# Decoder block with a PEER expert layer: gate factors applied by ScalarE, the search's small tables in PSUM, all 128 dot products in the first table stage

## The chip, the cores and the metric

The kernel runs on one core of one Trainium2 chip. The metric is the device time of one execution in microseconds, as the median of several runs; lower is better.

## What is computed

One layer for 512 tokens of width 1024, all in float32: RMSNorm, a combined projection, two mixers (HGRN2 and forgetting attention), a gated merge, and then the PEER layer, which the change touches:

```python
q = (xt @ w_q).reshape(T, PEER_HEADS, 2, PEER_DK_HALF)            # 8 heads, 2 halves
s = jnp.einsum('thpd,hpnd->thpn', q, sub_keys)                    # 128 keys per half
s1, i1 = lax.top_k(s[:, :, 0], 16)
s2, i2 = lax.top_k(s[:, :, 1], 16)
cand = (s1[..., :, None] + s2[..., None, :]).reshape(T, PEER_HEADS, 256)
cand_idx = (i1[..., :, None] * 128 + i2[..., None, :]).reshape(T, PEER_HEADS, 256)
top_s, pos = lax.top_k(cand, 16)
idx = jnp.take_along_axis(cand_idx, pos, axis=-1)                 # 16 of 16384 experts per head
gates = jax.nn.softmax(top_s, axis=-1)
a = jax.nn.gelu(jnp.einsum('cd,ced->ce', xc, u_table[ic]), approximate=False) * gc
y = jnp.einsum('ce,ced->cd', a, v_table[ic])                      # 128 experts per token
```

The result is h + y, normalised once more.

## The kernel before, in words

Four blocks follow one another, each closed by a barrier of all engines: the projections and mixers (to about 390 us), the merge and the queries of the search (to 600 us), **the first table stage** (to about 1285 us) and **the value stage** (to the end).

The tokens are in four tiles of 128. For three of them (384 tokens, `DT`) the PEER layer is dense: all 16384 experts are computed. In the first table stage TensorE goes through the table `u` in 128 *chunks* of 128 experts; chunk `j` is 24 products of 384 columns (`unit_product`, L212 to L214: every float32 operand is split into a high and a low part, and three products are summed per 128 rows). A unit of 512 KB is loaded by the SP queue into one of four buffers (`load_unit`), ScalarE copies out its high part (`split_hi`, L203), GpSimd subtracts to get the low part (`split_lo`, L207), four chunks ahead of TensorE (`LEAD`); the buffer of a chunk's split is that of the chunk that has just ended. ScalarE applies the gelu (L1169) and stores the result to memory. In the value stage the gelus times the dense gates are multiplied with the table `v`, again in 128 chunks; there VectorE makes the low parts.

The *dense gates* (for each token a 128x128 table of the 16 x 8 selected experts with their gates) are also made in the first table stage, in 96 *quads* of four tokens. For one token it is a product of two one-hot tables of 128 slots by 128 keys: `hot` (first key index) and `hotg` (second index, times the gate). VectorE makes both (`quads`, L1217 and four times L1223), comparing `iota` (0 to 127, in PSUM bank 3) with the indices in `slot_t`; TensorE multiplies them (L1380) right behind the chunk that `quad_chunk(q)` names; ScalarE moves the result out (L1177) and stores it in batches of eight quads (`dense_d`). Four quads can be under way (`HOTS`).

Where `slot_t` comes from is the *search* on VectorE. `retrieve_pair` does two heads of a tile: top 16 of four lists of 128 keys, the sums of candidates, top 16 of these, then the ranks (`rank`, L1281, L1282, and L1284 to `rank_f`), a comparison of ranks against `iota` (`pick`, L1286), its product with the key numbers (`key_f`, written by L1271, read by L1292) and a sum. There are 16 such *pairs*, four for each of the four tiles. After each tile ScalarE takes the exponential (at chunk `EXP_AT`), VectorE normalises (`normalise`), TensorE transposes (at chunk `SLOTS_AT`), and VectorE copies to `slot_t` (`slots_out`).

The fourth tile (the first one that is searched) is sparse: its 128 tokens gather their own 128 rows of `u` and 128 rows of `v` (`gather`, an indirect DMA from GpSimd's queue, L1046, 512 KB each, into six buffers). A *dot* (`u_dot`, L1055) multiplies one row buffer with the tokens' vectors, which stand in PSUM (`x_rows`), and sums up; a row of `v` is added by `add_row` in the value stage. 104 dots run in the first table stage (`DOTS_U`), 24 in the value stage, on a copy of the vectors in SBUF (`xs`). The gelu and the gates of the first 96 come at the end of the first stage, the rest at chunks 26 and 30 of the value stage.

The order of all this is written out by hand. Dots and quads are filled in between the dependent steps of a pair (`fill`; the numbers per pair are `PAIR_DOTS` and `PAIR_QUADS`), and the rest stands behind the last pair as a tail of two quads and two dots in turn. Gather `g` is issued by GpSimd behind its split of chunk `GATHER_AT[g]`. At chunk `MIX_AT` the SP queue loads the first two parts of what the value stage needs (`mix`).

## Time and profile before

| | us |
|---|---|
| median of 3 runs | 1870.97 |
| lowest, highest | 1869.51, 1871.16 |
| the profiled execution's own time | 1871.95 |
| its span, first to last instruction | 1870.1 |
| TensorE busy | 1766.6 (94%) |
| VectorE busy | 1327.5 (71%) |
| GpSimd busy | 821.1 (44%) |
| ScalarE busy | 669.9 (36%) |

The busy time of TensorE is modelled, since products are pipelined, so 94% is not nearness to its peak. The shares are means over stages with different limits, and the views by stretch tell more. "Idle before" stands with the instruction that ended the idle time, and with what it waited for. PEclk is the share of full TensorE clock (2.4 GHz) that was granted.

### The profile page before, as it was taken

To read this page: it belongs to the slowest core of one execution; us is meant where nothing else is said; L and a number is where in the kernel's file an instruction comes from. 1 tells how busy PE (TensorE), PEld (TensorE's weight loads), DVE (VectorE), ACT (ScalarE), POOL (GpSimd) and SP (SyncE) were. 2 spreads that over 40 slices of the span, in tenths; PEclk is the share of its full clock that TensorE was granted. 3 is DMA by queue.
4 is the path that set the end of the run, shared out by engine and by line. 5 is a ranking of instruction groups with operands and counts; after the bars stand their busy time and mean duration, and the time that the engine had idled before them with its cause. 6 is when DMAs were issued, how large, how long until landed. Compare 5 with 4: busy or idle time off the path is not lost. (4 is left out here: it accounts for less than half of the span.)

```text
span 1870.1 us, 25727 instructions
## 1 busy us (share of the span) xinstructions
PE 1766.6 (94%) x9603; PEld 1628.3 (87%) x9603; DVE 1327.5 (71%) x2720; ACT 669.9 (36%) x993; POOL 821.1 (44%) x478
## 2 busy tenths in 40 slices
PE   6998999999999999999999879885999999999997
PEld 4887876677788999989999878785999999999996
DVE  6467452644432699999999957761788888888885
ACT  4343333443321334334343324232333333333332
POOL 4432222234342787866555446454233334344420
PEclk8999999999999999999999989897999999999999
DMA  6322222255344788967677558777899999999991
GB/s 182 93 76 60 79 80 68 68 161 148 101 131 126 235 284 287 299 227 265 239 269 269 184 215 330 263 273 265 314 369 376 370 375 365 371 367 379 372 346 46
DMA packets 260844, 436.09 MB, mean 233 GB/s; under 512 B 14960, under 2 KB 184176, under 8 KB 259056
## 3 DMA queue, kind: packets, MB, share of 16 engines
q1 hardware_dynamic: 203696, 249.87, 41.0%
q0 software_dynamic: 36864, 134.23, 18.8%
q10 hardware_dynamic: 20160, 50.34, 7.3%
q8 instruction: 77, 1.26, 0.3%
q14 instruction: 47, 0.39, 0.1%
HBM read 373.57 MB, written 60.82 MB: 232 GB/s over the span
## 5 line engine op out<-in xcount | busy, mean ns | idle before, releaser
L207 POOL TENSOR_TENSOR spl_a<-raw,spl_a 128x1024 fp32r<-128x1024 f32 x172 | 419.4, 2439 | 477.2 <-ACT spl_a L203 472.8
L203 ACT ACTIVATE spl_a<-raw 128x1024 fp32r<-128x1024 f32 x296 | 313.1, 1059 | 538.2 <-PE bank L214 422.4
L212 PE MATMUL bank<-act,spl_a 128*128 128x384 f32 (+1 forms) x1216 | 433.1, 356 | 12.5 <-DVE act L480 7.7
L213 PE MATMUL bank<-act,spl_a 128*128 128x384 f32 (+1 forms) x1216 | 422.8, 348 | 0.0
L214 PE MATMUL bank<-act,spl_a 128*128 128x384 f32 (+1 forms) x1216 | 422.4, 347 | 0.0
L1046 POOL DMA_INDIRECT rows<-in_v_tab,expert x128 | 173.7, 1357 | 261.7 <-DVE acc L1498 231.4
L212 PE MATMUL bank<-aws,spl_a 128*128 128x384 f32 x768 | 260.4, 339 | 20.3 <-DVE aws L1484 20.3
L213 PE MATMUL bank<-aws,spl_a 128*128 128x384 f32 x768 | 260.2, 339 | 0.0
L214 PE MATMUL bank<-aws,spl_a 128*128 128x384 f32 x768 | 260.1, 339 | 0.0
L212 PEld LDWEIGHTS bank<-act,spl_a 128*128 128x128 f32 x1216 | 233.1, 192 | 24.7 <-issue 12.2
L213 PEld LDWEIGHTS bank<-act,spl_a 128*128 128x128 f32 x1216 | 233.0, 192 | 7.9 <-issue 1.0
L214 PEld LDWEIGHTS bank<-act,spl_a 128*128 128x128 f32 x1216 | 232.3, 191 | 8.2
L207 DVE TENSOR_TENSOR spl_a<-raw,spl_a 128x1024 fp32r<-128x1024 f32 x124 | 151.8, 1224 | 79.5 <-ACT spl_a L203 79.3
L1055 DVE SCALAR_TENSOR_TENSOR rows<-rows,x_rows 128x1024 f32<-128x1024 f32 x104 | 125.2, 1210 | 60.1 <-DMA rows<-in_u_rows,expert 59.9
L1046 POOL DMA_INDIRECT rows<-in_u_rows,expert x128 | 130.3, 1018 | 79.8 <-DVE rows L1055 59.3
L212 PEld LDWEIGHTS bank<-aws,spl_a 128*128 128x128 f32 x768 | 144.8, 189 | 20.6 <-issue 20.6
L207 POOL TENSOR_TENSOR spl_b<-raw,spl_b 128x1024 fp32r<-128x1024 f32 x37 | 90.4, 2449 | 163.3 <-ACT spl_b L203 163.3
L1498 DVE SCALAR_TENSOR_TENSOR acc<-rows,a_row,acc 128x1024 f32<-128x1024 f32 x126 | 159.1, 1279 | 0.0
L1452 ACT ACTIVATE aws<-aw 128x384 fp32r<-128x384 f32 x128 | 67.3, 526 | 228.8 <-DVE aw L1478 228.8
L214 PEld LDWEIGHTS bank<-aws,spl_a 128*128 128x128 f32 x768 | 144.8, 189 | 0.0
L213 PEld LDWEIGHTS bank<-aws,spl_a 128*128 128x128 f32 x768 | 144.8, 188 | 0.0
L1380 PE MATMUL bank<-hotg,hot 128*128 128x128 f32 x768 | 106.0, 289 | 37.2 <-DVE hotg L1223 37.2
(281 smaller groups left out, 2878.3 us busy)
## 6 DMA issues: line engine op xcount, KB each, us to landing
raw<-in_u_t SPq DMA_DIRECT2D x128, 512.0 KB, 4.1
raw<-in_v_tab SPq DMA_DIRECT2D x128, 512.0 KB, 7.2
gelu_ux<-gl ACTq DMA_DIRECT2D x128, 192.0 KB, 4.7
dense_gates<-mixbuf ACTq DMA_DIRECT2D x12, 2048.0 KB, 7.6
mixbuf<-dense_gates SPq DMA_DIRECT2D x32, 768.0 KB, 9.9
mixbuf<-gelu_ux SPq DMA_DIRECT2D x32, 768.0 KB, 12.6
raw<-in_w_in SPq DMA_DIRECT2D x45, 512.0 KB, 3.9
raw<-in_w_q SPq DMA_DIRECT2D x16, 512.0 KB, 4.0
```

Source lines behind the costliest of these rows:

```text
L203: eng.activation(spl(n, 0, slice(0, W)), raw[:, s, :], ACT.Copy).then_inc(hi_done, 1)
L207: eng.tensor_tensor(spl(n, 1, slice(0, W)), raw[:, n % RAW, :], spl(n, 0, slice(0, W)).bitcast(F32), ALU.subtract).then_inc(lo_done, 1)
L212: nc.tensor.matmul(out, w_hi, x_hi, start=first, stop=False)
L213: nc.tensor.matmul(out, w_hi, x_lo, start=False, stop=False)
L214: return nc.tensor.matmul(out, w_lo, x_hi, start=False, stop=last)
L1046: pool.indirect_dma_start(out=rows[:, g % ROWS, :], out_offset=None, in_=u_rows[:, :] if g < SLOTS else v_rows, in_offset=bass.IndirectOff ...
L1055: dve.scalar_tensor_tensor(out=row, in0=row, scalar=1.0, in1=x, op0=ALU.mult, op1=ALU.mult, accum_out=z_row[:, g:g + 1]).then_inc(row_used, 1)
L1380: ins = nc.tensor.matmul(bank[4 + q % 2][:, t * P:(t + 1) * P], hot[:, q % HOTS, t, :], hotg[:, q % HOTS, t, :], start=True, stop=True)
L1452: act_e.activation(aws[:, 0, j % 4, :], aw[:, j % 2, :], ACT.Copy).then_inc(a_hi, 1)
L1498: dve.scalar_tensor_tensor(out=acc[:, s % 2, :], in0=row, scalar=a_row[:, s:s + 1], in1=acc[:, s % 2, :], op0=ALU.mult, op1=ALU.add) \
```

## The change

Five things are changed together.

- `hotg` is gone as a tile of its own. `hot` has both halves, and VectorE makes both for a quad in one operation of 1024 elements, without gates. ScalarE then multiplies the second half with the gates, token by token, four Copy activations a quad with a factor from `slot_t` (new semaphore `hotg_ready`). It does so at the end of its work for the chunk before the quad's; TensorE waits for that.
- `rank` and `key_f` stand in PSUM bank 3 beside `iota`, no longer in SBUF.
- All 128 dots are done in the first table stage. `xs`, the late gelu and the late gates are gone; the value stage adds rows only. 134 gathers instead of 110 stand in the first table stage.
- `normalise` of a tile is called within the next tile's first pair, in the fourth of its eight fills.
- The tables of the order are new: quads, exponentials and transposes at earlier chunks (the last quad at 116 instead of 120), more dots per pair, `MIX_AT` 121 instead of 124.

```diff
-            hot = sb(ctx, "hot", [P, HOTS, QUAD, NK])
-            hotg = sb(ctx, "hotg", [P, HOTS, QUAD, NK])
+            hot = sb(ctx, "hot", [P, HOTS, 2, QUAD, NK])
...
+            def small(at):
+                return bank[3][:, at:at + 4 * TOPK]
+
             iota = bank[3][:, 0:P]
-            EXP_AT = [24, 48, 75, 102]
-            SLOTS_AT = [None, 51, 79, 103]
...
-            MIX_AT = 124
-            PAIR_DOTS = [0, 3, 4, 4, 5, 5, 5, 5, 5, 4, 4, 4, 4, 4, 4, 4]
+            rank = small(P).bitcast(U32).rearrange("p (a s k) -> p a s k", a=2, s=2)
+            key_f = small(P + 4 * TOPK).rearrange("p (a s k) -> p a s k", a=2, s=2)
...
+            EXP_AT = [24, 46, 69, 91]
+            SLOTS_AT = [None, 48, 72, 91]
...
+                         78, 78, 80, 81, 82, 83, 84, 85, 86, 87, 88, 89, 90, 91, 91, 91, 92, 92, 95, 95, 96, 96,
+                         97, 97, 98, 98, 99, 99, 100, 100, 101, 101, 103, 103, 105, 105, 106, 106, 108, 108, 110,
+                         110, 111, 111, 113, 113, 114, 114, 116, 116, 117, 117, 118, 118, 118, 118, 119, 119, 119,
+                         119, 121, 121, 123, 123, 124, 124]
+            MIX_AT = 121
+            PAIR_DOTS = [0, 3, 4, 4, 6, 6, 6, 6, 6, 5, 5, 5, 5, 5, 5, 5]
...
                 if q < 32:
-                    return 55 + 3 * q // 4
-                return 83 + 19 * (q - 32) // 32 if q < 64 else 105 + (q - 64) // 2
+                    return 52 + 22 * q // 32
+                return 75 + 17 * (q - 32) // 32 if q < 64 else 93 + 3 * (q - 64) // 4
...
+                    for q in range(NQUAD):
+                        if quad_chunk(q) == j + 1:
+                            act_e.wait_ge(hot_ready, q + 1)
+                            for t in range(QUAD):
+                                col = q * QUAD + t
+                                ins = act_e.activation(hot[:, q % HOTS, 1, t, :], hot[:, q % HOTS, 1, t, :],
+                                                       ACT.Copy, scale=slot_t[:, 2, col:col + 1])
+                            ins.then_inc(hotg_ready, 1)
                     act_e.wait_ge(z_free, j + 1)
                     act_e.dma_start(gelu_d[j, :, :], gl[:, j % 4, :]).then_inc(gelu_stored[j % 4], 16)
                     if j == NC - 2:
-                        act_e.wait_ge(row_used, GATED_U)
-                        act_e.activation(a_row[:, 0:GATED_U], z_row[:, 0:GATED_U], ACT.Gelu).then_inc(z_gelu, 1)
+                        act_e.wait_ge(row_used, SLOTS)
+                        act_e.activation(a_row[:, :], z_row[:, :], ACT.Gelu).then_inc(z_gelu, 1)
...
-                        dve.tensor_tensor(hot[:, q % HOTS, :, :],
-                                          iota.unsqueeze(1).to_broadcast([P, QUAD, NK]),
-                                          slot_t[:, 0, q * QUAD:(q + 1) * QUAD].unsqueeze(2)
-                                          .to_broadcast([P, QUAD, NK]), ALU.is_equal)
-                        for t in range(QUAD):
-                            col = q * QUAD + t
-                            ins = dve.tensor_scalar(hotg[:, q % HOTS, t, :], iota, slot_t[:, 1, col:col + 1],
-                                                    slot_t[:, 2, col:col + 1], ALU.is_equal, ALU.mult)
-                        ins.then_inc(hot_ready, 1)
+                        cols = slice(q * QUAD, (q + 1) * QUAD)
+                        dve.tensor_tensor(hot[:, q % HOTS, :, :, :],
+                                          iota.unsqueeze(1).unsqueeze(1).to_broadcast([P, 2, QUAD, NK]),
+                                          slot_t[:, 0:2, cols].unsqueeze(3).to_broadcast([P, 2, QUAD, NK]),
+                                          ALU.is_equal).then_inc(hot_ready, 1)
...
+                    if m % 4 == 0 and m and x == 3:
+                        normalise(m // 4 - 1)
...
-                for _ in range(2):
-                    quads(4)
-                    dots(2)
+                quads(8)
+                dots(2)
                 normalise(NT - 1)
                 dots(2)
                 slots_out(NT - 1)
-                for _ in range(15):
+                for _ in range(16):
                     quads(2)
                     dots(2)
-                quads(2)
-                dots(DOTS_U - made[0])
+                dots(SLOTS - made[0])
...
-                        pe.wait_ge(hot_ready, q + 1)
+                        pe.wait_ge(hotg_ready, q + 1)
...
-                    for g in range(min(ITEMS, j * ITEMS // ITEM_STEPS),
-                                   min(ITEMS, (j + 1) * ITEMS // ITEM_STEPS)):
-                        if DOTS_U + g < SLOTS:
-                            u_dot(dve, DOTS_U + g, xs[:, :])
-                        else:
-                            add_row(DOTS_U + g)
+                    for s in range(min(SLOTS, j * SLOTS // ROW_STEPS), min(SLOTS, (j + 1) * SLOTS // ROW_STEPS)):
+                        add_row(SLOTS + s)
```

How it moves the order. On VectorE, at the start of the first pair of the third tile (pair 9 of 0 to 15), before:

```order
L1241 MAX top_v<-scb 128x8 x4
L1217 TENSOR_TENSOR hot<-bank,slot_t 128x512
L1223 TENSOR_SCALAR hotg<-bank,slot_t 128x128 x4
L1246 MAX_INDEX top_i<-top_v,scb 128x8 x4
L1248 MATCH_REPLACE knock<-top_v,scb 128x128 x4
L1217 TENSOR_TENSOR hot<-bank,slot_t 128x512
L1223 TENSOR_SCALAR hotg<-bank,slot_t 128x128 x4
L1055 SCALAR_TENSOR_TENSOR rows,z_row<-rows,x_rows 128x1024
```

And in the changed kernel (`bank` is PSUM: `iota`, `rank` and `key_f` appear under that name):

```order
L1249 MAX top_v<-scb 128x8 x4
L1228 TENSOR_TENSOR hot<-bank,slot_t 128x1024
L1254 MAX_INDEX top_i<-top_v,scb 128x8 x4
L1256 MATCH_REPLACE knock<-top_v,scb 128x128 x4
L1228 TENSOR_TENSOR hot<-bank,slot_t 128x1024
L1055 SCALAR_TENSOR_TENSOR rows,z_row<-rows,x_rows 128x1024
```

The same steps stand between the same quads and dots; a quad is one operation instead of five.

On ScalarE, a chunk with two quads and the next one's split, before:

```order
L203 ACTIVATE spl_a<-raw 128x1024
L1169 ACTIVATE gl<-bank 128x384
L1177 ACTIVATE mixbuf<-bank 128x128x4 x2
L1185 DMA gelu_ux<-gl 128x384
L203 ACTIVATE spl_a<-raw 128x1024
```

And in the changed kernel:

```order
L203 ACTIVATE spl_a<-raw 128x1024
L1171 ACTIVATE gl<-bank 128x384
L1179 ACTIVATE mixbuf<-bank 128x128x4 x2
L1191 ACTIVATE hot<-hot,slot_t 128x128 x8
L1195 DMA gelu_ux<-gl 128x384
L203 ACTIVATE spl_a<-raw 128x1024
```

Eight factors for the two quads of the next chunk stand behind the evictions and ahead of the store and of the next split.

On GpSimd, the end of the first table stage, before:

```order
L1046 DMA rows<-in_u_rows,expert 128x1024 x2
L207 TENSOR_TENSOR spl_a<-raw,spl_a 128x1024 x4
L1046 DMA rows<-in_u_rows,expert 128x1024 x2
L207 TENSOR_TENSOR spl_a<-raw,spl_a 128x1024 x2
L1046 DMA rows<-in_u_rows,expert 128x1024 x2
L207 TENSOR_TENSOR spl_a<-raw,spl_a 128x1024
L1059 UNCONDITIONAL_BRANCH
```

And in the changed kernel:

```order
L1046 DMA rows<-in_u_rows,expert 128x1024 x4
L207 TENSOR_TENSOR spl_a<-raw,spl_a 128x1024
L1046 DMA rows<-in_u_rows,expert 128x1024 x4
L207 TENSOR_TENSOR spl_a<-raw,spl_a 128x1024 x2
L1046 DMA rows<-in_v_tab,expert 128x1024 x2
L207 TENSOR_TENSOR spl_a<-raw,spl_a 128x1024 x2
L1046 DMA rows<-in_v_tab,expert 128x1024 x2
L207 TENSOR_TENSOR spl_a<-raw,spl_a 128x1024
L1046 DMA rows<-in_v_tab,expert 128x1024 x2
L207 TENSOR_TENSOR spl_a<-raw,spl_a 128x1024 x3
L1059 UNCONDITIONAL_BRANCH
```

The last eight rows of `u` stand in two groups of four, six rows of `v` follow in this stage, and three splits instead of one stand behind the last gather.

## Rows read from the trace of the kernel before

**Rows 1.** Busy time by stretch: us, then PE, PEld, DVE, ACT, POOL busy, clock, DMA

```profile
1100.00:1200.00 100.00, 88.41 (x520) 86.41 (x521) 66.62 (x156) 34.72 (x53) 54.45 (x37) 0.91 0.73 273
...
1325.00:1500.00 175.00, 175.00 (x996) 175.00 (x995) 148.82 (x197) 65.96 (x84) 62.90 (x53) 1.00 1.02 375
```

**Rows 2.** One line, L212: TensorE, ns min/median/max, first and last start

```profile
L212 PE MATMUL bank<-act,spl_a x1024: 331/334/668, 600.5 to 1284.7; 128*128 128x384 f32 x171
```

**Rows 3.** Timeline of ScalarE, first table stage: start us, us, instruction, idle before

```profile
890.73 1.06 ACT L203 ACTIVATE spl_a<-raw 128x1024 fp32r<-128x1024 f32 x1 [3.13 <-PE bank L214]
891.69 0.47 ACT L1169 ACTIVATE gl<-bank 128x384 f32<-128x384 f32 x1
892.06 0.59 ACT L1177 ACTIVATE mixbuf<-bank 128x512 f32<-128x512 f32 x1
892.46 0.33 ACTq L1185 DMA_DIRECT2D gelu_ux<-gl  x1
...
896.68 1.06 ACT L203 ACTIVATE spl_a<-raw 128x1024 fp32r<-128x1024 f32 x1 [3.54 <-PE bank L214]
...
1277.19 1.06 ACT L203 ACTIVATE spl_a<-raw 128x1024 fp32r<-128x1024 f32 x1 [2.72 <-PE bank L214]
...
1281.35 1.06 ACT L203 ACTIVATE spl_a<-raw 128x1024 fp32r<-128x1024 f32 x1 [2.72 <-PE bank L214]
```

**Rows 4.** Waits from 600 to 1300: total us, times, longest

```profile
DVE rows L1055 <- DMA rows<-in_u_rows,expert: 59.9, 16, 13.1
...
PE bank L1380 <- DVE hotg L1223: 37.2, 21, 7.3
...
ACT spl_a L203 <- DMA raw<-in_v_tab: 7.2, 1, 7.2
```

**Rows 5.** Timelines of GpSimd, VectorE and TensorE around the end of the first stage

```profile
1291.86 2.34 POOL L207 TENSOR_TENSOR spl_a<-raw,spl_a 128x1024 fp32r<-128x1024 f32 x1 [4.02 <-ACT spl_a L203]
...
1303.54 1.03 DVE L1478 TENSOR_TENSOR aw<-mixbuf 128x384 f32<-128x384 f32 x2 [17.94 <-PEq L1059]
...
1305.69 0.66 PE L212 MATMUL bank<-aws,spl_a 128*128 128x384 f32 x1 [20.27 <-DVE aws L1484]
```

**Rows 6.** VectorE's groups from 600 to 1300: count, busy us, mean ns, idle before

```profile
L1223 DVE TENSOR_SCALAR hotg<-bank,slot_t 128x128 f32<-128x128 f32 x384 | 130.1, 399 | 0.0
L1055 DVE SCALAR_TENSOR_TENSOR rows<-rows,x_rows 128x1024 f32<-128x1024 f32 x104 | 125.2, 1210 | 60.1 <-DMA rows<-in_u_rows,expert 59.9
L1217 DVE TENSOR_TENSOR hot<-bank,slot_t 128x512 f32<-128x512 f32 x96 | 65.1, 678 | 2.1 <-PE bank L1380 2.1
L1292 DVE TENSOR_TENSOR pick<-pick,key_f 128x1024 f32<-128x1024 f32 x16 | 31.1, 1946 | 0.1
...
L1271 DVE CAST key_f<-top_i 128x64 f32<-128x64 uint32 x16 | 14.6, 915 | 0.6
...
L1281 DVE TENSOR_SCALAR rank<-pair_i 128x32 uint32<-128x32 uint32 x16 | 12.6, 786 | 0.5
```

**Rows 7.** The lines of four search operations: ns min/median/max

```profile
L1292 DVE TENSOR_TENSOR pick<-pick,key_f x16: 1209/1831/3039, 619.7 to 1073.5; 128x1024 f32<-128x1024 f32 x16
...
L1271 DVE CAST key_f<-top_i x16: 195/454/2570, 611.3 to 1057.4; 128x64 f32<-128x64 uint32 x16
...
L1281 DVE TENSOR_SCALAR rank<-pair_i x16: 181/446/2107, 617.9 to 1070.0; 128x32 uint32<-128x32 uint32 x16
...
L1286 DVE TENSOR_TENSOR pick<-rank_f,bank x16: 1220/1222/1223, 618.4 to 1070.5; 128x1024 f32<-128x1024 f32 x16
```

**Rows 8.** A group of ScalarE before 600 us: busy us, mean ns

```profile
L364 ACT ACTIVATE off_k<-kc 128x128 f32<-128x128 f32 x12 | 3.9, 389 | 0.0
```

**Rows 9.** Timeline of VectorE: the first operation of pair 14 and of pair 15

```profile
1010.42 0.87 DVE L1241 MAX8 top_v<-scb 128x8 f32<-128x128 f32 x4
...
1045.83 0.87 DVE L1241 MAX8 top_v<-scb 128x8 f32<-128x128 f32 x4
```

**Rows 10.** DMA issues, gathered rows of u: count, median us to landing

```profile
rows<-in_u_rows,expert POOLq DMA_INDIRECT x128, 6.1
```

More of the change, by code:

```diff
@@ L88 @@
 HOTS = 4
-DOTS_U = 104
-GATED_U = 96
 def exp_events(e):
@@ L1339, in _ @@
                         if i and p == 1:
-                            normalise(i - 1) if i == 1 else None
                             slots_out(i - 1)
@@ L1344, in _ @@
                             expert_rows(p)
-                        elif p == 0 and i > 1:
-                            normalise(i - 1)
-                            dots(1)
                     shift(i)
-                for _ in range(2):
-                    quads(4)
-                    dots(2)
+                quads(8)
+                dots(2)
                 normalise(NT - 1)
@@ L1444, in _ @@
             def _(act_e):
-                act_e.activation(xs[:, :], x_rows[:, :, :].rearrange("p b t -> p (b t)"), ACT.Copy) \
-                    .then_inc(xs_ready, 1)
                 def weight_hi(j):
@@ L1490, in add_row @@
                     row = rows[:, g % ROWS, :]
-                    dve.wait_ge(a_ready, 1 if s < GATED_U else 2)
                     dve.wait_ge(row_in[g % ROWS], 16 * (g // ROWS + 1))
@@ L1505, in _ @@
                 weight_lo(1)
-                dve.wait_ge(xs_ready, 1)
+                dve.wait_ge(a_ready, 1)
                 for j in range(NC):
@@ L1548, in _ @@
                     for d in range(KD):
-                        if j == 0 and d == 6:
-                            pe.wait_ge(xs_ready, 1)
                         c = slice(d * P, (d + 1) * P)
```

29 lines of the change are left out of this document (8 added, 21 removed), and 7 rows, old and new, of the table GATHER_AT.

## The prediction

> **What bounds the kernel now.** I read the page first, then the busy time by stretch, then who waited for whom, and last the rows of single engines. TensorE is the engine to watch. In the value stage it has no gap at all: busy 175.00 of 175.00 us at full clock [rows 1], so nothing that happens to other engines there can shorten it. The lost time lies before it. The first table stage starts its first product at 600.5 and its last at 1284.7 [rows 2]. What that stage costs at full pace comes from ScalarE, which splits one unit after each chunk: 1281.35 minus 1277.19 is 4.16 us for a chunk with no quad, and 896.68 minus 890.73 is 5.95 for a chunk with two, so a quad of dense-gate products costs 0.89 [rows 3]. 128 chunks and 96 quads make 532.5 + 85.9 = 618.4 us. The stage took 1285.1 - 600.5 = 684.6, which is **66 us too much**.
>
> Who holds TensorE up is in the waits: its gate products waited 37.2 us for VectorE's gate tables, in 21 pieces, and VectorE itself waited 59.9 us for gathered rows [rows 4]. In the stretch from 1100 to 1200, TensorE was idle for 11.6 us and its clock was 0.91 of full on the mean; some parts ran at the lower level (1.2 of 2.4 GHz), so 9 us more went to the clock [rows 1]. A us of waiting costs up to about 0.8 us again in clock. Then comes the turn between the stages: TensorE is idle for 20.27 us [rows 5].
>
> **The change, part by part.**
>
> *One-hot tables.* A quad now costs VectorE one table operation of 512 elements (678 ns) and four gate-table operations, together (65.1 + 130.1) / 96 = 2.03 us. The new single operation has 1024 elements, one input in PSUM and one in SBUF, both broadcast; the candidate comparison L1286 is of that size and sort and takes 1.22 us each time [rows 6, 7]. 96 x (2.03 - 1.22) = 78 us less on VectorE.
>
> *Gate factors on ScalarE.* No row has a Copy with a factor from SBUF. The nearest is L364, 128x128 with a per-partition bias: 389 ns alone, and 3.9 us busy for twelve, 0.33 each in a row [rows 8]. The bounds are that 0.33, and 0.39 if nothing overlaps; I take 0.33, so 1.3 us for a quad. In a chunk with two quads ScalarE then has 1.06 (split) + 0.47 (gelu) + 1.1 (two evictions) + 2.6 = 5.2 of 5.95 us [rows 3, 8]. It fits, with 0.7 us over. What is queued behind the new wait for the table is the store of the gelu and, in the next chunk, the split; split units are four chunks ahead of TensorE, so a wait of a few us there costs nothing. It adds 1.3 us between VectorE's table and TensorE.
>
> *Small tables in PSUM.* The operation L1292 takes 1209 ns at best and 1946 on the mean, L1271 195 and 915, L1281 181 and 786 [rows 6, 7]. The same data and the same work, so the difference is waiting, while GpSimd splits units. L1286, with an input in PSUM, shows no such spread (1220 to 1223). The excess is 0.74 + 0.72 + 0.61 = 2.1 us a pair, 33 us in 16 pairs. I take it as gone; the bounds are 0 and 33. A rule speaks against this part. L1286 with PSUM data takes 1222 ns and L1292 at its best, all in SBUF, 1209 [rows 7]: 13 ns between them. The Trainium skill (VectorE: DVE Perf Modes, section on the TRN2 errata) gives 120 cycles of fixed cost for a source in PSUM and 58 for one in SBUF; by it I would add about 65 ns to four operations in 16 pairs, 4 us of VectorE's time, as an estimate.
>
> *All 128 dots in this stage.* 24 more dots at 1.21 us [rows 6] are 29 us more for VectorE. In the pairs there are ten more than before (76 against 66), and the last 16 stand behind the last quad, where nobody on TensorE waits. The 24 gathers that go with them stand in GpSimd's queue among its splits, four each at chunks 118 and 119.
>
> *What comes out for TensorE.* Pair 14 of before ran from 1010.42 to 1045.83, 35.4 us, with 8 quads and 4 dots [rows 9]. With the new operations it is 35.4 - 8 x 0.81 + 1.2 = 30.1 us for 8 quads and 5 dots, 3.8 us a quad. I hold that against TensorE's pace by chunk, 600.5 + 4.16 per chunk + 0.89 per quad. Quads 0 to 31 stand over chunks 52 to 73, 3.8 us each: VectorE just keeps up. The transposes of the second tile end with chunk 72, at about 932, so pair 13 starts near 935. Quads 32 to 63 stand over chunks 75 to 91, 3.1 us each: here TensorE is faster. Quad 55 comes at 935 + 3 x 30.1 - 1 + 1.3 = 1025, and chunk 87 wants it at 600.5 + 88 x 4.16 + 55 x 0.89 = 1016. **9 us of waiting** remain. From quad 64 on VectorE needs 2 x (1.22 + 1.21) = 4.9 us for two quads and two dots, and TensorE 8 us for the two; the gathers come four to eight chunks ahead of the quads behind them, where before it was two, and a row lands 6.1 us after its issue [rows 10]. I expect no waits there.  For the clock I take 3.5 us, half of what the ratio above makes of 9 us, bounds 0 and 7.
>
> *The turn.* Before, ScalarE's last split waited 7.2 us for its unit of the value table, which the SP queue issues behind the first two parts of the mix [rows 4]. That put GpSimd's last split at 1291.86 to 1294.2, and VectorE, held at the block's end, went on at 1303.54 [rows 5]: 9.3 us that no row explains, while gathers were under way. The mix is now issued three chunks earlier, 12 us, and the last gathers two chunks earlier. GpSimd's last split should then end about 3.5 us behind TensorE's last product instead of 9. From VectorE's restart to the first product it is 2.2 us. The unexplained part is bounded by 0 and 9.3; I take 5, its middle, since nothing says what it waits for. 3.5 + 5 + 2.2 = 10.7, so 9.5 less (5 to 14.5).
>
> *The value stage.* VectorE does 24 dots less and the queue of gathers is shorter by 24, beside a TensorE that was never idle there: 0.
>
> *Sum.* The profiled execution took 1871.95 us, 1.0 above the median of the runs. 1871.95 - 66 + 9 + 3.5 - 9.5 = 1809; as much below the median's scale as the rounding of a term, so **1809** stands.
>
> **The rivals.**
>
> *A. The small tables save nothing*, since the waits beside GpSimd stay or turn up in other operations. For it: the cast L1271 has only 64 elements and waits just as long as L1292, so size is not the cause and the place of one operand may not be either. Against it: the steady 1220 to 1223 of L1286. Then every pair is 2.1 us longer, from the first to quad 55 some 15 of them; less what VectorE would else wait for an exponential, quad 55 comes some 25 us later: **1834**. By the Trainium skill (SBUF — State Buffer, section Who interferes with whom) a VectorE instruction with at most one SBUF input and outside its two-port modes does not contend with GpSimd; by that rule this rival is out.
>
> *B. The rows come late in the last third*, as before: GpSimd has 2.4 us of split and four gathers of 0.95 to 1.3 in a chunk of 4.16, each needs a freed buffer, and the split behind them is late for TensorE. For it: 59.9 us of such waits before. Against it: the lead of four chunks. At a quarter of the 37.2 us of before, with 0.8 of it again for the clock, it is 16 us: **1825**.
>
> *C. ScalarE becomes the bound, slower than before.* In its queue a table with factors stands ahead of the next split and gelu. At x us per factor, a quad chunk (65 of them, 1.48 quads each) costs it 1.06 + 0.47 + 0.33 (issuing the store) + 1.48 x (0.55 + 4x), against TensorE's 5.48. It decides from x = 0.47, and eats the whole gain from 0.66; at 0.7 the 65 chunks lose 1.4 us each, 90 us, in place of the 9 + 3.5 us: **1887**. Nothing in the trace is as dear: 0.39 at most [rows 8]. The Trainium skill (ScalarE: Activation LUTs, Rules for kernel authors) says to use VectorE, not ScalarE, for mul: by it this part should not pay.
>
> **How the numbers follow.** The forecast has 0.60, A 0.16, B 0.14, C 0.06, and 0.04 is left for a stall that gives just about all back. The range reaches down to 1792 (no stall, no clock loss, a turn of 6 us) and up to 1838, behind A. A measurement here tells 0.2%, 4 us, from nothing. Faster: 0.60 + 0.16 + 0.14 = 0.90; same 0.03; slower 0.07.
>
> **What would show it.** Right, step by step: the new table operation at 1.22 us x96; the three small-table operations with their mean at their least; factors at 0.39 with 1.3 us a quad; the wait of the gate products under 15 us and now for ScalarE, around 990 to 1030; the last first-stage product near 1232; TensorE's gap at the turn near 11; the value stage as long as before. Wrong: a mean of L1292 that stays over 1.5 us (A); waits for gathered rows behind quad 64 with TensorE idle (B); ScalarE busy over nine tenths between 940 and 1180 (C); or gaps in the value stage, which would make its term not zero.

## The result: 1827.7 us, and the profile after

The changed kernel takes **1827.7 us** (median of 4, 1824.6 to 1828.9) against 1871.1 us (median of 4 in the same measurement): a ratio of 0.976, interval 0.975 to 0.978. The forecast was 1809, in a range from 1792 to 1838. The profiled execution took 1824.62 with a span of 1822.5, so it is 47.3 us below the 1871.95 of the one before, where the sum said 63.

First the ends of the first table stage (its first product, then the line of the unit products), and TensorE's first product behind the turn:

```profile
599.99 0.41 PE L212 MATMUL bank<-act,spl_a 128*128 128x384 f32 x1 [1.79 <-PEq L776]
```

```profile
L212 PE MATMUL bank<-act,spl_a x1216: 334/334/792, 20.8 to 1250.1; 128*128 128x384 f32 x146, 128*128 128x512 f32 x28
```

```profile
1258.66 0.66 PE L212 MATMUL bank<-aws,spl_a 128*128 128x384 f32 x1 [7.92 <-DVE aws L1476]
```

The stage began at 600.0, and its last product ended 7.92 us before 1258.66, at 1250.7: 650.8 us. Read the same way, the stage of before ran from 600.5 to 1305.69 - 20.27 = 1285.4 [rows 5], 684.9 us; the 684.6 of the prediction took the end of the last product of L212, 0.3 us earlier. The idle time behind the stage is 7.9 us, where it was 20.27. The value stage is 544.6 us long (545.2 before). So 34.2 of the 47.6 us of span came from the first stage and 12.3 from the turn, and only 0.6 from the value stage; the blocks ahead of the stage were 0.5 us shorter.

The busy time by stretch, with columns as in [rows 1]:

```profile
940.00:1060.00 120.00, 108.69 (x710) 107.10 (x709) 99.01 (x242) 84.17 (x202) 63.95 (x38) 1.00 0.72 264
1060.00:1228.40 168.40, 168.40 (x1062) 168.09 (x1060) 94.89 (x129) 99.18 (x224) 120.60 (x79) 1.00 0.93 349
1228.40:1240.80 12.40, 0.01 (x1) 0.03 (x1) 0.00 (x0) 1.44 (x2) 2.87 (x4) 0.71 1.06 405
1240.80:1262.00 21.20, 13.28 (x59) 12.99 (x59) 5.17 (x8) 6.13 (x10) 12.03 (x7) 0.74 0.60 197
...
1325.00:1500.00 175.00, 175.00 (x998) 175.00 (x997) 141.36 (x168) 65.97 (x83) 46.27 (x44) 1.00 0.99 348
```

For 168 us behind 1060 TensorE has no gap. Then it does nothing for 12.4 us, while the DMA engines are busy 1.06 of the time (the share counts packets that overlap) and move 405 GB/s. The waits that answer to [rows 4], from 600 to 1300:

```profile
DVE rows L1055 <- DMA rows<-in_u_rows,expert: 72.1, 31, 16.0
...
ACT spl_a L203 <- DMA raw<-in_v_tab: 17.6, 1, 17.6
PE bank L212 <- ACT gl L1171: 13.5, 3, 12.4
...
PE bank L1382 <- ACT hot L1191: 9.2, 7, 3.1
```

The 12.4 us are one wait for a gelu, and the gelu was late because the split ahead of it in ScalarE's queue waited 17.6 us for a unit of the value table. The gate products waited 9.2 us instead of 37.2.

VectorE's groups, which answer to [rows 6]:

```profile
L1055 DVE SCALAR_TENSOR_TENSOR rows<-rows,x_rows 128x1024 f32<-128x1024 f32 x128 | 154.5, 1213 | 72.3 <-DMA rows<-in_u_rows,expert 72.1
L1228 DVE TENSOR_TENSOR hot<-bank,slot_t 128x1024 f32<-128x1024 f32 x96 | 115.0, 1213 | 24.7 <-PE bank L1382 24.6
L1280 DVE TENSOR_TENSOR cand<-top_v 128x512 f32<-128x512 f32 x16 | 21.5, 1344 | 0.0
...
L1300 DVE TENSOR_TENSOR pick<-pick,bank 128x1024 f32<-128x1024 f32 x16 | 19.5, 1217 | 0.1
...
L1279 DVE CAST bank<-top_i 128x64 f32<-128x64 uint32 x16 | 3.6, 228 | 0.6
...
L1289 DVE TENSOR_SCALAR bank<-pair_i 128x32 uint32<-128x32 uint32 x16 | 3.1, 195 | 0.5
```

The three small-table operations are at 1217, 228 and 195 ns, near their least of before [rows 7]. But the operation that makes the candidate sums, `cand`, with both inputs in SBUF, rose:

```profile
L1272 DVE TENSOR_TENSOR cand<-top_v 128x512 f32<-128x512 f32 x16 | 13.1, 821 | 0.0
```

That is its row of the kernel before: 821 ns, now 1344. ScalarE's factors:

```profile
L1191 ACT ACTIVATE hot<-hot,slot_t 128x128 f32<-128x128 f32 x384 | 120.2, 397 | 28.3 <-DVE hot L1228 25.9 <-ACT mixbuf L1179 2.4
```

**Where the last 14 us of the stage went.** I held the start of chunks against 4.16 us a chunk and 0.89 a quad. At chunk 75 TensorE is 4.2 us late, at chunk 93 it is 18.4, at chunk 125 it is 18.7, at chunk 126 31.2 and at chunk 127 32.7. The jump is the stall, 12.4 us, and behind it 1.6 us of slow products: the first eight took 0.52 to 0.66 us each and not 0.33, and the granted clock from 1240.8 to 1262 is 0.74. The SyncE queue at that place:

```profile
1211.91 0.38 SPq L1031 DMA_DIRECT2D mixbuf<-dense_gates  x1
1212.34 8.11 SPq L1034 DMA_DIRECT2D mixbuf<-gelu_ux  x1
1220.50 1.77 SPq L1031 DMA_DIRECT2D mixbuf<-dense_gates  x1
1222.31 6.38 SPq L1034 DMA_DIRECT2D mixbuf<-gelu_ux  x1
1228.74 28.48 SPq L187 DMA_DIRECT2D raw<-in_v_tab  x8
```

Issuing the four pieces of the mix held the queue for 16.8 us, and the next unit was issued behind them, at 1228.7. It landed at 1239.2; ScalarE had waited for it since 1221.6. In the kernel before the same four took 8.8 us. The first reading was therefore: the mix stands in the wrong place, among the gathers of chunks 118 to 124.

### The profile page after: what moved, and what is told of

Read it like the earlier page. It is cut to its first block and busy times, and to the rows that moved or that the text cites. A ratio compares the mean times of both kernels' runs of the same rounds, so it can differ in the third digit from the quotient of the medians.

```text
span 1822.5 us, 25722 instructions
## 1 busy us (share of the span) xinstructions
PE 1748.1 (96%) x9603; PEld 1613.7 (89%) x9603; DVE 1229.6 (67%) x2335; ACT 780.0 (43%) x1375; POOL 773.4 (42%) x478
## 5 line engine op out<-in xcount | busy, mean ns | idle before, releaser
L207 POOL TENSOR_TENSOR spl_a<-raw,spl_a 128x1024 fp32r<-128x1024 f32 x172 | 414.2, 2410 | 417.5 <-ACT spl_a L203 416.0
L212 PE MATMUL bank<-act,spl_a 128*128 128x384 f32 (+1 forms) x1216 | 429.2, 353 | 24.7 <-ACT gl L1171 13.5
L1046 POOL DMA_INDIRECT rows<-in_v_tab,expert x128 | 137.4, 1073 | 370.9 <-DVE acc L1489 348.9
L212 PE MATMUL bank<-aws,spl_a 128*128 128x384 f32 x768 | 260.2, 339 | 7.9 <-DVE aws L1476 7.9
L212 PEld LDWEIGHTS bank<-act,spl_a 128*128 128x128 f32 x1216 | 230.2, 189 | 37.2 <-issue 24.5
L213 PEld LDWEIGHTS bank<-act,spl_a 128*128 128x128 f32 x1216 | 230.1, 189 | 7.8 <-issue 1.0
L214 PEld LDWEIGHTS bank<-act,spl_a 128*128 128x128 f32 x1216 | 229.7, 189 | 8.1
L1055 DVE SCALAR_TENSOR_TENSOR rows<-rows,x_rows 128x1024 f32<-128x1024 f32 x128 | 154.5, 1213 | 72.3 <-DMA rows<-in_u_rows,expert 72.1
L212 PEld LDWEIGHTS bank<-aws,spl_a 128*128 128x128 f32 x768 | 145.0, 189 | 8.2 <-issue 8.2
L1046 POOL DMA_INDIRECT rows<-in_u_rows,expert x128 | 123.9, 968 | 26.1 <-issue 15.2
L1191 ACT ACTIVATE hot<-hot,slot_t 128x128 f32<-128x128 f32 x384 | 120.2, 397 | 28.3 <-DVE hot L1228 25.9
```

What stands on the lines that cost most here:

```text
L207: eng.tensor_tensor(spl(n, 1, slice(0, W)), raw[:, n % RAW, :], spl(n, 0, slice(0, W)).bitcast(F32), ALU.subtract).then_inc(lo_done, 1)
L212: nc.tensor.matmul(out, w_hi, x_hi, start=first, stop=False)
L213: nc.tensor.matmul(out, w_hi, x_lo, start=False, stop=False)
L214: return nc.tensor.matmul(out, w_lo, x_hi, start=False, stop=last)
L1046: pool.indirect_dma_start(out=rows[:, g % ROWS, :], out_offset=None, in_=u_rows[:, :] if g < SLOTS else v_rows, in_offset=bass.IndirectOff ...
L1055: dve.scalar_tensor_tensor(out=row, in0=row, scalar=1.0, in1=x, op0=ALU.mult, op1=ALU.mult, accum_out=z_row[:, g:g + 1]).then_inc(row_used, 1)
```

## The experiments

Each ratio is to the kernel before, measured on the same chip in the same session; medians of kernels are compared with the 1827.7 of the changed kernel. The runs of one variant lie within 6.1 us of each other, those of the kernel before between 1868.4 and 1878.7 over the three sessions; its medians there are 1873.0 to 1873.7, against 1871.1 beside the changed kernel. A difference of 3 us between two variants therefore says nothing without their traces.

### The mix back at chunk 124

```diff
-            MIX_AT = 121
+            MIX_AT = 124
```

> The changed kernel with one number other: the four expert mixes of the turn are issued at chunk 124, as in the kernel before, and not at 121. Theory: the idle 12.4 us of TensorE at 1228 to 1241 us of the changed kernel come from the mixes standing on SyncE's queue between the gathers of chunks 118 to 121, where issuing them holds the queue 16.9 us and the unit loads behind them come late. Then the wait of TensorE before the first piece of chunk 126 or so shrinks from 12.4 us to under 3, the four issues hold the queue under 10 us, and the time is 8 to 14 us under the changed kernel's 1827.7 (about 1816). Rival: the gathers of rows in chunks 118 to 124 alone take the bandwidth, whatever stands beside them; then a stall of 9 us or more stays and the time is within 4 us of 1827.7. Second rival: the mixes at 124 are late for the turn; then the gap between the last product of the first stage and the first of the value stage grows from 7.9 us back toward 20.3, and the time is at 1827.7 or above.

Measured: 1823.7 us, ratio 0.975 (0.972 to 0.977). The stall before the end of the stage is gone: the last product ends at 1237.5, not 1250.7. But the gap at the turn is now 19.6 us, not 7.9.

```profile
1228.44 1.43 SPq L1034 DMA_DIRECT2D mixbuf<-gelu_ux  x1
1229.92 3.67 SPq L1031 DMA_DIRECT2D mixbuf<-dense_gates  x1
1233.63 6.67 SPq L1034 DMA_DIRECT2D mixbuf<-gelu_ux  x1
1240.35 15.35 SPq L187 DMA_DIRECT2D raw<-in_v_tab  x5
```

```profile
1249.33 1.06 ACT L203 ACTIVATE spl_a<-raw 128x1024 fp32r<-128x1024 f32 x1 [13.47 <-DMA raw<-in_v_tab]
```

The first fence is the SyncE queue, the second a row of ScalarE. The mix is again followed by a late unit, now the last one that GpSimd must split before the stage can end. **The theory falls.** 12.4 + 7.9 = 20.3 us became 0 + 19.6: a place only decides on which side of the turn the time is lost. The mechanism of the second rival came, though the time did not rise with it; that it fell by 4 us is hardly more than sessions differ by. What stays the same in both kernels is the DMA engines at a share of 1.0 or more from 1200 us on. That gave the second theory: the bytes that must land before the turn set the sum of the two gaps.

### Three ways to fewer bytes before the turn

The first leaves out the six gathers of value rows that stood in the first stage, the last entries of `GATHER_AT` (the rest of the list is as it was):

```diff
-                         119, 121, 121, 123, 123, 124, 124]
+                         119]
```

> The changed kernel without the six gathers of rows of the value table in chunks 119 to 124 of the first stage: they are issued at the value stage's start (128 gathers in the first stage and not 134). From 1200 to 1240 us of the changed kernel the DMA engines are full (share 1.03 to 1.06 at 395 to 414 GB/s), and moving the mixes to chunk 124 only moved the 20.3 us that TensorE is idle around the turn to another place. Theory (the turn is bound by the bytes that must land there): 3.1 MB less at 414 GB/s is 7.6 us less of idle TensorE, so the 12.4 + 7.9 us become about 13 and the time is 5 to 9 us under the changed kernel's. Rival (latency and order of the SyncE queue bind it, not bytes): the two gaps still sum to 18 us or more and the time is within 3 us.

Measured: 1821.5 us, ratio 0.972 (0.969 to 0.974), 6.2 less. The gaps are 7.4 + 7.4 = 14.8, so 5.5 less where 3.1 MB at 414 GB/s had said 7.6. (0.5 of the 5.5 is the turn's, and has another cause, below.)

The second issues the second mix, 1.5 MB, in the value stage:

```diff
                         mix(sp, 0)
-                        mix(sp, 1)
...
                     if n < N_UNITS:
                         load_unit(sp, n)
+                    if j == 0:
+                        mix(sp, 1)
```

> The changed kernel with mix 0 at chunk 121 as it is, and mix 1 (1.5 MB, used from piece 4 of the value stage on) issued after the first unit load of the value stage. Theory (bytes bind the turn): 1.57 MB less at 414 GB/s ahead of the turn is 3.8 us less of idle TensorE, and as two issues fewer stand on SyncE's queue ahead of the unit loads: the sum of the two gaps 20.3 goes to 14 to 17 and the time is 3 to 6 us under the changed kernel's. Rival (mix 1 is then late): a new wait of over 5 us before piece 4 of the value stage on mixbuf, and nothing gained.

Measured: 1821.2 us, ratio 0.972 (0.969 to 0.974), 6.5 less; the gaps are 5.7 + 7.9 = 13.6, and there is no new wait in the value stage. It gave more than its bytes do at 414 GB/s (3.8), so the place of the issues in SyncE's queue has a share too.

The third has 104 dots in the first stage, as before the change, with 110 gathers in place of 134:

```diff
+DOTS_U = 104
...
-                    dots(2)
-                dots(SLOTS - made[0])
+                    dots(min(2, DOTS_U - made[0]))
```

> The changed kernel with only 104 of the 128 dot products in the first stage and the last 24 in the value stage, as in the kernel before; tables in PSUM, factors on ScalarE, schedule of quads and mixes as in the changed kernel. Theory (bytes bind the turn; the 24 dots bought nothing): from 1200 to 1240 us some 18 gathers of 0.52 MB are gone, DMA share falls under 1, the idle 12.4 + 7.9 us of TensorE become 8 or less, and the time is 8 to 14 us under the changed kernel's. Rival (the move of the dots is worth time, since the value stage's VectorE had 24 items more and its waits): the value stage grows from 544.6 us by 2 or more, and the time is at or over the changed kernel's.

Measured: 1819.9 us, ratio 0.971 (0.969 to 0.973), 7.8 less and just short of the 8 to 14 expected. The value stage, with 24 dots more, is 1.4 us longer. The stall is gone, and the DMA share falls as said:

```profile
1228.40:1236.80 8.40, 8.40 (x49) 8.08 (x47) 1.49 (x1) 3.16 (x5) 4.80 (x2) 1.00 0.50 173
1240.00:1249.00 9.00, 0.00 (x0) 0.00 (x0) 0.00 (x0) 0.00 (x0) 0.38 (x1) 0.53 0.00 0
```

The second of these rows is the surprise. From 1240 to 1249 no engine works, but for the last 0.4 us of GpSimd's split, and **no byte moves**; the gap at the turn is 15.1 us. Bytes can't explain that one.

The same run tells how gathers and the queue hang together. The four pieces of the mix stand at the same place in SyncE's queue as in the changed kernel, and only the gathers beside them are fewer:

```profile
1207.75 0.38 SPq L1033 DMA_DIRECT2D mixbuf<-dense_gates  x1
1208.18 0.81 SPq L1036 DMA_DIRECT2D mixbuf<-gelu_ux  x1
1209.04 2.23 SPq L1033 DMA_DIRECT2D mixbuf<-dense_gates  x1
1211.31 3.78 SPq L1036 DMA_DIRECT2D mixbuf<-gelu_ux  x1
1215.14 1.92 SPq L189 DMA_DIRECT2D raw<-in_v_tab  x1
```

They held the queue for 7.4 us instead of 16.8. So the bytes act in good part through the queue: with 24 gathers less, the same issues take less than half the time, and the unit behind them is issued that much sooner.

### What the empty 9 us are

The rows stand under the line that opens the block, whose end all engines meet. DRAIN of GpSimd's sequencer there (count: ns min/median/max, start), of the changed kernel:

```profile
L1059 POOLq DRAIN  x1: 4587/4587/4587, 1251.9 to 1251.9; - x1
```

of the kernel before:

```profile
L1059 POOLq DRAIN  x1: 11445/11445/11445, 1291.8 to 1291.8; - x1
```

and of the kernel with 104 early dots:

```profile
L1061 POOLq DRAIN  x1: 11447/11447/11447, 1238.0 to 1238.0; - x1
```

It starts with GpSimd's last split and, with 110 gathers in the block, ends 9.07 us after it, to 2 ns the same in two kernels. This is the 9.3 us of [rows 5] for which the prediction found no row: the row was there, under the line of the block and not in GpSimd's busy time. In the other kernels it ended 2.21 us after the split with 134 gathers and 1.72 with 128. Two runs put numbers to it. They have 116 and 110 early dots, with six gathers more in each:

```diff
-DOTS_U = 104
+DOTS_U = 116
```

> The kernel of the run with 104 early dots, with 116 dots and 122 gathers in the first stage (12 more of each), all else the same. What holds the turn there is GpSimd's DRAIN at the block's end: it ends 9070 ns after GpSimd's last split with 110 gathers in the block, 2210 with 134, 1719 with 128, and at the end of the value stage 3184 with 146 and 1223 with 122. Theory (the DRAIN goes by the number of gathers in the block, with 82 ns for each from some number on, and it does not matter when they stand or whether DMA is busy): with 122 it ends 1.22 us after the last split, TensorE's gap at the turn is about 7.5 us instead of 15.4, and since 12 gathers less than in the changed kernel still leave no stall at the bytes, the time is 6 to 9 us under the 1819.9 of 104 dots (about 1812). Rival 1 (the DRAIN takes 9 us in blocks whose last gather is long past, as the 75 us there): the gap stays at 14 or more and nothing is gained. Rival 2 (12 gathers more bring the stall at the bytes back): a new idle stretch of 4 us or more before 1240 us.

Measured: 1810.3 us, ratio 0.966 (0.964 to 0.969), 9.6 under the kernel with 104; the gap at the turn is 7.2 us and no stall came back, though the DMA share was 0.97 (364 GB/s) from 1200 to 1237. In the changed kernel it was 1.05 (407 GB/s) from 1200 to 1240.

```profile
L1061 POOLq DRAIN  x1: 3608/3608/3608, 1238.4 to 1238.4; - x1
```

> The same with 110 dots and 116 gathers in the first stage. It tells on which side of the jump a block of 116 gathers stands: a DRAIN that ends 9.5 us after the last split (9070 + 6 x 82) and a time within 2 us of the 1819.9 of 104 dots, or one that ends 0.7 us after it (1223 - 6 x 82) and a time 7 to 10 us lower. If the DRAIN goes by something other than the count, its end is neither.

Measured: 1812.2 us (1809.5 to 1815.4), ratio 0.967 (0.964 to 0.969); the profile is that of the slowest run.

```profile
L1061 POOLq DRAIN  x1: 3118/3118/3118, 1243.4 to 1243.4; - x1
```

It ended 0.739 us after the last split, where 0.73 was expected. With the ends of both table stages there are seven counts: 110, 116, 122, 128, 134, 140 and 146 gathers give 9.07, 0.74, 1.22, 1.72, 2.21, 2.69 and 3.18 us. Every gather past 116 costs 82 ns, and 110 stands alone. Neither the time since the last gather (6 us before the end of the last split in the kernel before, 76 us with 104 dots) nor the DMA load (128 GB/s meanwhile, and none) changes it.

The runs so far that touch the turn, with one of below (quads spread). "Held" is the time from the first issue of the mix to the next unit's in SyncE's queue:

| run | gathers in the stage | held, us | stall before the end, us | gap at the turn, us |
|---|---|---|---|---|
| changed kernel | 134 | 16.8 | 12.4 | 7.9 |
| mix at 124 | 134 | 12.3 | 0 | 19.6 |
| no early rows | 128 | 15.2 | 7.4 | 7.4 |
| second mix in the value stage | 134 | 8.4 (two issues) | 5.7 | 7.9 |
| quads spread | 134 | 18.5 | 11.9 | 7.9 |
| 116 dots | 122 | 9.7 | 0 | 7.2 |
| 110 dots | 116 | 6.5 | 0 | 6.8 |
| 104 dots | 110 | 7.4 | 0 | 15.1 |

### Undoing the other two parts

Rank and key table back in SBUF:

```diff
-            rank = small(P).bitcast(U32).rearrange("p (a s k) -> p a s k", a=2, s=2)
-            key_f = small(P + 4 * TOPK).rearrange("p (a s k) -> p a s k", a=2, s=2)
+            rank = sb(ctx, "rank", [P, 2, 2, TOPK], U32)
+            key_f = sb(ctx, "key_f", [P, 2, 2, TOPK])
```

> The changed kernel with rank and key_f back in SBUF; PSUM holds only the iota. Theory (the tables in PSUM free VectorE of the waits in its operations with two inputs in SBUF): the rank comparisons go from 1215 ns back to the 1946 and 915 ns of before, VectorE's work grows by about 25 us in all over the pairs, and since VectorE is busy 98 us of 100 from 800 to 1000 us of the changed kernel, most of it goes to the end: 15 to 30 us over 1827.7 (about 1848). Rival (the saving is given back in the other operation, cand, which rose from 821 to 1344 ns, and in idle time): the time stays within 5 us of 1827.7.

Measured: 1844.6 us, ratio 0.985 (0.982 to 0.987): 16.9 slower than the changed kernel.

```profile
L1300 DVE TENSOR_TENSOR pick<-pick,key_f 128x1024 f32<-128x1024 f32 x16 | 29.9, 1871 | 0.1
...
L1279 DVE CAST key_f<-top_i 128x64 f32<-128x64 uint32 x16 | 20.4, 1273 | 0.5
...
L1289 DVE TENSOR_SCALAR rank<-pair_i 128x32 uint32<-128x32 uint32 x16 | 14.3, 891 | 0.5
...
L1280 DVE TENSOR_TENSOR cand<-top_v 128x512 f32<-128x512 f32 x16 | 10.9, 680 | 0.0
```

The waits return to the tables and leave `cand`, which is back at 680 ns. So VectorE's wait goes from operation to operation: the tables save 0.65 + 1.05 + 0.70 = 2.40 us a pair and `cand` takes back 0.66. Part of rival A is true.

What the wait is for stands in the timelines, one operation of VectorE beside one of GpSimd. First the changed kernel, then the kernel before:

```profile
823.92 2.39 POOL L207 TENSOR_TENSOR spl_a<-raw,spl_a 128x1024 fp32r<-128x1024 f32 x1 [0.65 <-ACT spl_a L203]
823.97 2.90 DVE L1280 TENSOR_TENSOR cand<-top_v 128x512 f32<-128x512 f32 x1
```

```profile
644.90 2.57 DVE L1271 CAST key_f<-top_i 128x64 f32<-128x64 uint32 x1
645.00 2.40 POOL L207 TENSOR_TENSOR spl_a<-raw,spl_a 128x1024 fp32r<-128x1024 f32 x1
```

`cand` ends 0.55 us behind the split, the cast 0.06. That is so for every one of these operations that took over 0.25 us more than its least. In the kernel before and in this run, the cast and the shift (L1281, here L1289) end 0.04 to 0.06 us behind a split, and the product 1.08 or 1.09; in the changed kernel `cand` ends 0.55 or 0.56 behind one. The Trainium skill (SBUF — State Buffer, Who interferes with whom) says that VectorE and GpSimd contend for one shared pair of ports, held as an exclusive lock. The rows agree: the other engine's operation has to end first. What has an input in PSUM is steady at 1217 to 1221, and the product and `cand`, with both in SBUF, pick up the wait. Two inputs are not needed for it: the cast and the shift have a single one and waited as long as they also wrote to SBUF (here 1273 and 891 ns on the mean, 195 and 181 at best).

VectorE makes the gate factors again:

```diff
-                            for t in range(QUAD):
-                                col = q * QUAD + t
-                                ins = act_e.activation(hot[:, q % HOTS, 1, t, :], hot[:, q % HOTS, 1, t, :],
-                                                       ACT.Copy, scale=slot_t[:, 2, col:col + 1])
...
+                        for t in range(QUAD):
+                            col = q * QUAD + t
+                            ins = dve.tensor_scalar(hot[:, q % HOTS, 1, t, :], iota, slot_t[:, 1, col:col + 1],
+                                                    slot_t[:, 2, col:col + 1], ALU.is_equal, ALU.mult)
```

> The changed kernel with VectorE making the gated tables as before (one table operation of 128x512 and four of 128x128 per quad) and no factor operations on ScalarE; schedule, PSUM tables and all 128 dot products as in the changed kernel. Theory (the factors on ScalarE carry the larger share of the gain): VectorE gets back 96 x (0.68 + 4 x 0.40 - 1.20) = about 103 us of work; from 600 to 1228 us it had 499.5 of 658.7 us busy, so its 80 idle us between 1060 and 1228 take part of it and 30 to 70 us go to the end: 1855 to 1900. Rival (the PSUM tables and the earlier dots carry it, and the factors are bought from slack): within 10 us of 1827.7.

Measured: 1859.3 us, ratio 0.993 (0.991 to 0.995): 31.6 slower. VectorE is the bound from 940 to 1060, busy 118.80 of 120:

```profile
940.00:1060.00 120.00, 102.58 (x605) 100.50 (x605) 118.80 (x363) 37.10 (x59) 52.33 (x31) 0.91 0.62 222
```

The Trainium skill (ScalarE: Activation LUTs, Rules for kernel authors) would have the multiplication on VectorE. This run says no for this kernel: what counts is which engine is full.

Twice the factors on ScalarE, to see how far the next bound is (into a tile `spare`, with a wait for the quad before):

```diff
+                                act_e.activation(spare[:, t, :], hot[:, q % HOTS, 1, t, :],
+                                                 ACT.Copy, scale=slot_t[:, 2, col:col + 1])
```

> The changed kernel with the 384 gate-factor operations of ScalarE issued twice, the first time into a tile that nobody reads: 4 x 0.31 us = 1.25 us more of ScalarE per quad. Theory (ScalarE still has room now, but is the next bound): per chunk 1.52 us of split and gelu plus 1.82 us per quad is 4.2, 4.9 and 3.9 us of some 5.4 in the three runs of quads; doubled it is 6.0, 7.3 and 5.6 us, which is over the chunk by 0.6 x 22, 1.9 x 17 and 0.3 x 24 us: some 50 us slower than 1827.7 (1865 to 1890). If the factors still lie wholly beside other work: under 8 us slower. If ScalarE were already the bound in all three runs: 96 x 1.25 = 120 us slower.

Measured: 1864.8 us, ratio 0.996 (0.995 to 0.997): 37 slower, where the sum per chunk said some 50.

```profile
940.00:1060.00 120.00, 106.10 (x672) 103.16 (x670) 106.71 (x254) 110.86 (x308) 57.00 (x34) 0.99 0.68 243
1060.00:1250.00 190.00, 175.75 (x1092) 172.84 (x1092) 93.63 (x125) 154.50 (x402) 120.00 (x79) 0.99 0.82 301
```

ScalarE is busy 110.86 of 120 and the gate products wait for it. Rival C's way of failing is real; the actual factor, at 0.31 us in a row, is half of what this run has, and where between the two ScalarE begins to decide was not measured. In this run, as in the two before it, the gaps around the turn are 12.4 and 7.9 us, wherever the stage's end lies: they don't depend on what VectorE and ScalarE had to do earlier.

### Quads spread over more chunks

```diff
-                return 75 + 17 * (q - 32) // 32 if q < 64 else 93 + 3 * (q - 64) // 4
+                return 75 + 20 * (q - 32) // 32 if q < 64 else 96 + 11 * (q - 64) // 16
```

> The changed kernel with quads 32 to 63 placed over chunks 75 to 94 (not 75 to 91) and quads 64 to 95 over chunks 96 to 117 (not 93 to 116). In the changed kernel chunks 80 to 92 took some 13 us more than their products, TensorE waiting 9.2 us for ScalarE's factors, which wait for VectorE's tables; VectorE is busy 59.5 of 60 us from 940 to 1000. Theory (VectorE sets that pace, and with three chunks more TensorE has other products to do meanwhile): the waits of TensorE for hot go from 9.2 us to under 3, and the time falls by 5 to 10 us. Rival (the saving comes back at the turn, where bytes bind): the waits for hot fall as said, but the gaps at the turn grow by as much and the time is within 3 us of the changed kernel's.

Measured: 1821.1 us, ratio 0.971 (0.969 to 0.974), 6.6 less, in the 5 to 10 expected. The waits for the factors fall to one of 0.8 us; the transposes of the last tile wait 4.6 us for VectorE where it was 2.9. The gaps at the turn are as they were (11.9 + 7.9), so the saving held and was not taken back there.

### A kernel faster than both

Tables in PSUM, factors on ScalarE, and then: quads spread, second mix in the value stage, 116 dots and 122 gathers in the first stage, and the last exponential and transposes of the search at chunks 89 and 92:

```diff
-            EXP_AT = [24, 46, 69, 91]
-            SLOTS_AT = [None, 48, 72, 91]
+            EXP_AT = [24, 46, 69, 89]
+            SLOTS_AT = [None, 48, 72, 92]
```

> The candidate for a kernel faster than both: tables in PSUM and factors on ScalarE as in the changed kernel; quads 32 to 63 over chunks 75 to 94 and 64 to 95 over 96 to 117; 116 dots and 122 gathers in the first stage; mix 1 after the first unit load of the value stage; the third exponential of the search at chunk 89 and its transposes at chunk 92 instead of 91 both. From the run with spread quads (1821.1): the stall at the bytes 12.3 us goes, the wait for the transposes 4.6 us goes, the DRAIN is 1.0 us shorter: 1803, up to 1809 if half of the clock's share stays. If the stall at the bytes stays or the mix comes late: 1815 or more.

Measured: **1800.6 us** (median of 5, 1799.4 to 1801.0), ratio 0.961 (0.959 to 0.963), 27 below the changed kernel and 2 below the least that was expected.

```profile
940.00:1060.00 120.00, 118.25 (x775) 117.74 (x774) 106.33 (x250) 87.26 (x207) 71.56 (x43) 1.00 0.83 301
1060.00:1225.00 165.00, 165.00 (x1044) 165.00 (x1043) 74.53 (x98) 100.29 (x227) 112.91 (x69) 1.00 0.90 330
```

```profile
1232.98 0.66 PE L214 MATMUL bank<-aws,spl_a 128*128 128x384 f32 x1 [7.23 <-DVE aws L1483]
```

The first stage is 7.0 us over its pace, and there is no stall at its end. What is left besides is the 7.2 us at the turn. The earlier exponential and the later transposes had no run of their own, so their share is not known.

## Why the prediction was right, and where it was not

The sign, the range and the main mechanism held: the gate products no longer wait 37 us for VectorE. By its own steps:

- *One-hot tables*: forecast 1.22 us, measured 1213 ns. *Factors*: forecast 1.3 us a quad, measured 1.25. *Value stage*: forecast 0, measured -0.6.
- *Small tables*: taken as 2.1 us a pair, 33 in all, "I take it as gone". Gone for the three, but 8.4 of it came back in `cand`, which had no term; both its inputs are in SBUF, so the sentence that put rival A out did not reach it. The cast to `rank_f`, from 508 to 224 ns, gave 4.5 that nobody had forecast. Undoing the part costs 16.9 us of time.
- *Waiting around quad 55*, forecast 9 us: between chunks 75 and 93 the gate products waited 8.4 us for the factors, as forecast. But TensorE was 4.2 us late at chunk 75 already ("VectorE just keeps up" had 0), and it waited 2.9 us at chunk 91 for the transposes of the last tile, which had no term: VectorE stood 10.3 us for the exponential that ScalarE makes at that same chunk. From 75 to 93 it lost 14.2 us, 11.3 of them idle; the other 2.9 have no row. The clock in that stretch stayed at 1.00, so its 3.5 us were not needed. In all 18.7 where 12.5 was forecast. The agreement on the 8.4 is in part luck: the pair of 35.4 us that the sum starts from held a wait of 2.2 us in `cand` (2908 ns where 684 is usual), so that pairs took 28.6 to 28.8 and not 30.1, while pair 13 began at 938.8 and not at 935.
- *ScalarE's room*: "0.7 us over" left out the 0.33 us of issuing the store, which rival C's sum has. It was enough all the same.
- *The turn*: forecast 3.5 + 5 + 2.2 = 10.7, measured 3.6 + 2.5 + 1.8 = 7.9. The unexplained part, put at the middle of 0 and 9.3, was the DRAIN (9.07 of the 9.3), and fell to 2.5 since 134 gathers are not 110. That the turn came out near its forecast is luck: nothing in the prediction said that the number of gathers counts, and with 110 of them, as in the run with 104 dots, it is 9.3 again.
- **The step that failed** is "The mix is now issued three chunks earlier, 12 us, and the last gathers two chunks earlier", which the turn counted as pure gain, beside "I expect no waits there" for the stage from quad 64 on. That held for the gate products, but the sum had no term for a late unit. The prediction weighed queues and latencies and never summed the bytes. With 24 gathers more and both mixes in the same 40 us, the DMA engines are full, issuing the mix holds the queue for 16.8 us, and TensorE stands still for 12.4 us and is slow for 1.6 more: 14.0 us of the 15.6 by which the profiled execution exceeds the forecast. The rest of the stage adds 5.3, and the turn and the other blocks take 3.7 back. Rival B had the right resource in the wrong place: it looked for late gathered rows, and of the 72.1 us of such waits on VectorE 53.1 fell behind 1060, where TensorE had no gap up to the stall.

So the third part of the change, all 128 dots in the first stage, did not pay: with 104 the kernel is 7.8 us faster, with 116 17.4. The other two carry the gain, 16.9 and 31.6 us when undone alone. Their sum less 7.8 is 40.7, near the 43.4 of the whole, but the parts need not add up: each was undone under the new order of quads. That new order and the moved `normalise` had no run of their own.

What stays open: the order in SyncE's queue and the bytes were not told apart cleanly, since the run that moved the second mix changed both. Bytes at 414 GB/s give neither the 5.5 us of the run without early rows (7.6 by bytes) nor the 6.7 of the run with the second mix later (3.8 by bytes). And the jump of the DRAIN lies somewhere between 110 and 116 gathers.

## What to carry to other kernels

When a change takes compute off the path, add up the bytes that must land in the stretch that is left, at the highest rate the trace shows, before calling any transfer early enough. If two gaps keep nearly the same sum wherever you put an operation, its place alone is not the cause. And an idle stretch in which no engine and no DMA works has its row among the instructions that don't count as busy: read those at a block's end too, one engine at a time.

## What the runs showed of the hardware

- GpSimd's DRAIN at the end of a block goes by the number of indirect gathers in it: 82 ns for each from 116 to 146, 0.74 us to 3.18 us after its last operation, and 9.07 us at 110. 9.07 is 111 times 82 ns and 0.74 is 9 times, which looks like a store of some hundred entries that is emptied when full; that is a guess, and no run looked at what is counted.
- Around the turn the 16 DMA engines moved 372 to 417 GB/s in stretches of 10 us at a share over 1 (395 to 414 in the changed kernel, 372 to 417 with the mix at 124). In the Trainium skill (DMA: Bandwidth & Descriptors, Where 436 GB/s comes from) the fabric's ceiling is 435 GB/s and that of one core's memory traffic about 358; this kernel, alone on its chip, goes well over the second and stays under the first.
- With the DMA engines full, issuing one transfer of gelus from SyncE held its queue for 8.1 and 6.4 us, against 0.7 and 4.8 before the change and 0.8 and 3.8 with 24 gathers less. A late issue thus delays every load behind it.
- A 128x64 cast with its output in PSUM took 228 ns and one with its input there 224, where the first took 195 at best in SBUF; the 1024-element product with one input in PSUM took 1217 against 1209.
- An operation of VectorE with inputs and output in SBUF that waits for a split of GpSimd ends a fixed time behind the split's end: 0.04 to 0.06 us for a 128x64 cast and a 128x32 shift, 0.55 for a 128x512 sum, 1.08 for a 128x1024 product. The other way round GpSimd waits: a split that began 0.1 us behind such a product took 3.38 us instead of 2.40.
- ScalarE's 128x128 Copy with a factor from SBUF took 397 ns on the mean, and since neighbours overlap, 0.31 us of busy time each.
